# Turning paged keys on another engine: a decoder step's score stage rebuilt around a ring of sixteen half-page slots

## What is computed

```python
k_past = cache_k[page_table].reshape(nb, -1, N_HEADS, HEAD_DIM)     # 8 x 2048 x 16 x 64, fp32
v_past = cache_v[page_table].reshape(nb, -1, N_HEADS, HEAD_DIM)
F_all = cumsum(concatenate([lf_past, lf_s], axis=1), axis=1)
s = einsum('nqhd,nkhd->nhqk', q, k) * HEAD_DIM ** -0.5 + fq - fk
p = softmax(where(kpos <= qpos, s, -inf))
o = einsum('nhqk,nkhd->nqhd', p, v)
x = x + (o * silu(z)) @ w_out
```

## Time and profile before

| | |
|---|---|
| median of 3 runs | 979.52 us (976.55 to 979.72) |
| span of the profiled execution | 973.7 us, 23729 instructions |
| TensorE busy | 935.6 us, 96% |
| VectorE, ScalarE, GpSimd busy | 489.1, 384.8, 168.3 us |
| moved by DMA | 206.4 MB |

### The profile page before, as it was taken

The page is one execution under the profiler, slowest core; times in us unless marked ns, Lnnn a source line. Parts: engine busy times, 40 slices in busy tenths (PEclk is TensorE's granted clock), DMA queues, the critical chain, the costliest instruction groups (busy, mean ns, idle before and its releaser), DMA issues.

```text
span 973.7 us, 23729 instructions
## 1 busy us (share of the span) xinstructions
PE 935.6 (96%) x8516; PEld 798.8 (82%) x8516; DVE 489.1 (50%) x1133; ACT 384.8 (40%) x728; POOL 168.3 (17%) x111
## 2 busy tenths in 40 slices
PE   3899999999999999999999999999999999999998
PEld 2899999999998997758768768678687687786898
DVE  5744645555256434453554544644535545545732
ACT  5233333332135443453543544535435445436210
POOL 2243444331130221101102002012020020100000
PEclk8799999999999999999999999999999999999999
DMA  6222222322542525879799799798897997986412
GB/s 211 68 85 86 66 87 84 86 86 89 152 150 81 177 87 178 295 253 368 249 334 335 241 361 317 245 372 297 280 356 251 352 336 241 370 317 227 166 44 98
DMA packets 133188, 206.40 MB, mean 212 GB/s; under 512 B 8831, under 2 KB 91312, under 8 KB 133026
## 3 DMA queue, kind: packets, MB, share of 16 engines
q1 hardware_dynamic: 123538, 199.40, 60.7%
q10 hardware_dynamic: 9088, 4.46, 1.7%
q0 software_dynamic: 528, 2.10, 0.8%
HBM read 195.29 MB, written 10.63 MB: 211 GB/s over the span
## 4 chain that ended last, share of the span: by engine, by line
PE 84%; DMA 5%; DVE 4%; ACT 4%; issue 2%; SPq 0%; ACTq 0%; DVEq 0%
PE psum L1224 41%; PE psum L1194 17%; PE psum L1249 9%; PE psum L1382 7%; PE psum L1497 4%; DMA page_ring<-in_cache_k 4%; ACT sample_scores L708 2%; PE psum L1447 2%; DMA w_raw<-in_a_w_out 1%; PE psum L1425 1%; PE psum L1297 1%; PE psum L1405 1%; PE psum L1427 1%; PE psum L1429 1%; DMA constants<-in_table 0%
## 5 line engine op out<-in xcount | busy, mean ns | idle before, releaser
L1224 PE MATMUL psum<-xn_high,w_high 128*128 128x256 f32 x992 | 233.9, 318 | 2.6 <-DVE xn_low L821 2.6
L1224 PE MATMUL psum<-xn_low,w_high 128*128 128x256 f32 x992 | 213.6, 297 | 0.0
L1224 PE MATMUL psum<-xn_high,w_low 128*128 128x256 f32 x992 | 213.5, 297 | 0.0
L1224 PEld LDWEIGHTS psum<-xn_high,w_high 128*128 128x128 f32 x992 | 162.9, 191 | 19.6 <-issue 16.6
L1224 PEld LDWEIGHTS psum<-xn_high,w_low 128*128 128x128 f32 x992 | 168.1, 190 | 0.0
L1224 PEld LDWEIGHTS psum<-xn_low,w_high 128*128 128x128 f32 x992 | 168.0, 190 | 0.0
L1194 PE MATMUL psum<-constants,page_ring 128*128 128x128 f32 x1024 | 136.4, 276 | 6.3 <-DMA page_ring<-in_cache_k 5.0
L1194 PEld LDWEIGHTS psum<-constants,page_ring 128*128 128x128 f32 x1024 | 114.1, 140 | 33.4 <-issue 31.9
L503 POOL TENSOR_TENSOR w_raw<-w_raw,gains 128x1024 f32<-128x1024 f32 x32 | 60.7, 1897 | 339.2 <-DMA w_raw<-in_b_w_in 218.3
L1002 DVE COPY k_turned_odd<-psum 128x512 f32<-128x512 f32 x64 | 44.1, 690 | 93.1 <-PE psum L1194 93.1
L835 DVE TENSOR_TENSOR w_low<-w_raw,w_high 128x1024 fp32r<-128x1024 f32 x32 | 49.6, 1551 | 78.7 <-ACT w_high L565 78.7
(11 more groups left out here) (236 smaller groups left out, 1418.7 us busy)
## 6 DMA issues: line engine op xcount, KB each, us to landing
page_ring<-in_cache_k SPq DMA_DIRECT2D x128, 512.0 KB, 5.6
page_ring<-in_cache_v SPq DMA_DIRECT2D x128, 512.0 KB, 4.7
w_raw<-in_a_w_in SPq DMA_DIRECT2D x32, 512.0 KB, 4.0
suffix<-suffix_scratch SPq DMA_DIRECT2D x32, 256.0 KB, 4.6
w_raw<-in_b_w_in SPq DMA_DIRECT2D x16, 512.0 KB, 5.6
w_raw<-in_kv_w SPq DMA_DIRECT2D x16, 512.0 KB, 6.3
w_raw<-in_a_w_out SPq DMA_DIRECT2D x4, 1024.0 KB, 5.0
f_broad<-f_scratch SPq DMA_DIRECT2D x8, 512.0 KB, 6.0
```

Source lines behind the costliest of these rows:

```text
L1224: mm = pe.matmul(PS[:, bank + h, 0:c.stop - c.start], w[:, k, :], x[:, k, c], start=(k == 0 and n == 0), stop=(k == KT - 1 and n == 2))
```

## The change

- Key pages are no longer turned by PE. DVE turns them in place, in blocks of 32 x 32 (`turn_keys`), one instruction per ring slot.
- The ring has 16 slots. A key slot holds the same half (8 heads) of two pages, loaded by two DMAs of 256 KB with a page number read for each; slots 0 to 7 hold the first half of the heads of all 16 pages, 8 to 15 the second half. A value slot holds one page as before.
- Scores come in two rounds (`past_scores`) of 64 matmuls of 32 x 32 tiles, 512 columns wide, into four PSUM banks. ACT spreads the queries (`spread`). The suffix is loaded straight into `SS` in one DMA of 1 MB, and four adds put the scores on it in place.
- Value slots 0 to 7 wait for round 0 (`b_scored`), 8 to 15 for round 1. The gate weights are loaded behind key slot 13 of the previous head.
- The high and low parts of the gated outputs of the prompt are made in the last head for all heads, instead of in each head. Buffers are moved, the mask of the new keys is loaded at the end, the spread of the queries for the new keys is made by POOL at the end.

```diff
-RING = 8
+RING = 16
+HALF_D = D // 2
@@ SP
+        def load_keys(b, n, free=None):
+            pages = [page_of(b, 2 * (n % 8) + e) for e in range(2)]
+            if free:
+                sp.wait_ge(*free)
+            for e in range(2):
+                src = kpages[bass.ds(pages[e], 1), :, n // 8 * HALF_D:(n // 8 + 1) * HALF_D]
+                sp.dma_start(ring[:, n, e * HALF_D:(e + 1) * HALF_D],
+                             src.rearrange("a p n -> (a p) n")).then_inc(b_page[n], 16)
...
         def heads(i, last):
-            for n in range(STREAM):
...
+            sp.wait_ge(b_c0f, 4 * i)
+            sp.wait_ge(b_c1f, 4 * i)
+            src = f_dram[bass.ds(2 * i, 2), 0:SEQ].unsqueeze(0).to_broadcast([P, 2, SEQ])
+            sp.dma_start(FB[:, :, :], src).then_inc(b_fb, 16)
+            if not last:
+                sp.wait_ge(b_split, KT + 3 * i + 1)
+                load_w(wkv, (i + 1 + KT) * P, 0)
+            for n in range(NPG):
+                load_values(i, n, (b_scored, 2 * i + n // 8 + 1) if n % 8 == 0 else None)
+                if n == 7 and not last:
+                    sp.wait_ge(b_split, KT + 3 * i + 3)
                     load_w(wkv, (i + 1) * P, 1)
...
+            for n in range(NPG):
...
+                    load_keys(i + 1, n, (b_used, NPG * i + n + 1))
+                if n == 8:
+                    sp.wait_ge(b_t0, 8 * i + 4)
+                    sp.wait_ge(b_t1, 8 * i + 4)
...
+                        load_suffix(i + 1)
+                if n == 13 and not last:
+                    sp.wait_ge(b_split, KT + 3 * i + 5)
+                    load_w(wqz, (i + 1 + KT) * P, 1)
@@ ACT, heads
+            pr, sa = both(D0)
+            act.wait_ge(b_proj, KT + 3 * i + 1)
...
+            act.activation(SQ[:, SEQ:TOK], sa, ACT.Square).then_inc(b_dact, 1)
+            high_b(KT + 3 * i + 2, 1)
...
+            if last:
+                act.wait_ge(b_used, NPG * i + 10)
+                for k in range(KT - 1):
+                    act.activation(G2H[:, k, 0:SEQ], QF[:, k, 0:SEQ], ACT.Copy).then_inc(b_gh, 1)
@@ DVE
+        def turn_keys(b, n):
+            dve.wait_ge(b_page[n], 48 * b + 32)
+            dve.transpose(ring[:, n, :], ring[:, n, :]).then_inc(b_turned, 1)
+
+        for n in range(4):
+            turn_keys(0, n)
@@ DVE, heads
+            for n in range(4, 8):
+                turn_keys(i, n)
+            dve.wait_ge(b_proj, KT + 3 * i + 1)
+            pr, sa = both(D0)
...
+            dve.tensor_scalar(KN_T[:, SEQ:TOK], sa, gk, None, ALU.mult).then_inc(b_ddve, 1)
+            low_b(KT + 3 * i + 2, 1)
+            for n in range(8, NPG):
+                turn_keys(i, n)
...
+            for g in range(4):
+                ss = SS[:, :].rearrange("p (n g k) -> p n g k", g=4, k=32)[:, :, g, :]
+                dve.tensor_tensor_reduce(ss, PS[:, T0 + g, :].rearrange("p (n k) -> p n k", k=32), ss,
+                                         1.0, NEG, ALU.add, ALU.max, TINY[:, 4 + g:5 + g]).then_inc(b_taken, 1)
...
             block_turned(2)
+            if not last:
+                turn_keys(i + 1, 0)
             block_divide(3)
+            if not last:
+                turn_keys(i + 1, 1)
...
                 low_b(KT + 3 * i + 4, 1)
+                turn_keys(i + 1, 2)
+                turn_keys(i + 1, 3)
...
+            if last:
+                for k in range(KT - 1):
+                    low(k).then_inc(b_gl, 1)
@@ PE, heads
+            def past_scores(r):
+                half = ring[:, 8 * r:8 * r + 8, :].rearrange("p s (e c) -> p (s e) c", e=2)
+                for e in range(2):
+                    for a in range(2):
+                        for j in range(4):
+                            for g in range(4):
+                                h, c = 2 * r + e, ((2 * j + e) * 2 + a) * 32
+                                mm = pe.matmul(
+                                    PS[32 * j:32 * j + 32, T0 + g, :].rearrange("p (n k) -> p n k", k=32),
+                                    QC[32 * g:32 * g + 32, j, 64 * h + 32 * a:64 * h + 32 * a + 32],
+                                    half[32 * g:32 * g + 32, :, c:c + 32],
+                                    start=(h == 0 and a == 0), stop=(h == 3 and a == 1), tile_position=(32 * g, 32 * j))
+                mm.then_inc(b_scored, 1)
...
+            project(0, range(KT - 1))
...
+            pe.wait_ge(b_turned, NPG * i + 8)
+            project(0, [KT - 1])
+            past_scores(0)
+            project(1, range(1))
...
+            project(1, range(1, KT - 1))
+            pe.wait_ge(b_turned, NPG * i + NPG)
+            project(1, [KT - 1])
+            past_scores(1)
```

More of the change, by code:

```diff
@@ L188, in build @@
     CO = place("conv_rows", [18, D], over=at["probs_t"])
-    WHB = place("w_high_b", [P, KT, SLAB], F32R, over=at["k_turned"])
+    WHB = place("w_high_b", [P, KT, SLAB], F32R, over=slot(14))
     WLB = place("w_low_b", [P, KT, SLAB], F32R, over=at["p_turned"])
@@ L198, in build @@
     QF = place("queries", [P, KT, TOK], over=at["gated_high"])
+    QZ = place("q_spread", [P, NB, KT, 32], over=at["sample_scores"])
     FA = place("f_raw", [H, TOK], over=at["k_t"])
@@ L203, in build @@
     FT = place("f_sum", [H, TOK], over=at["f_broad"])
-    SN = place("new_scores", [P, NB, NS], over=at["suffix"])
-    NBI = place("new_bias", [P, NB, NS], over=at["suffix"] + 4 * NB * NS)
+    SN = place("new_scores", [P, NB, NS], over=at["new_keys"])
+    NBI = place("new_bias", [P, NB, NS], over=at["new_keys"] + 4 * NB * NS)
     PNT = place("new_probs_t", [NS, NB, P], over=at["probs"])
@@ L366, in _ @@
             load_w(wqz, n * P, n % 2)
+        sp.wait_ge(s_rows, 16 * 9)
+        sp.wait_ge(s_cs, H)
+        for n in range(2):
+            load_keys(0, n)
         for t in range(NT):
@@ L370, in _ @@
             sp.dma_start(h_dram[t * P:t * P + rows(t), :], X[0:rows(t), t, :]).then_inc(s_hst, 16)
+        for n in range(2, 7):
+            load_keys(0, n)
         sp.wait_ge(s_co, 1)
@@ L384, in _ @@
         sp.wait_ge(s_xl, 2 * NT)
-        for n in range(RING // 2):
-            load_page(0, n)
+        for n in range(7, 9):
+            load_keys(0, n)
         sp.wait_ge(s_ft, 1)
@@ L512, in heads @@
             scale_b(1, 6 + 2 * i, G_B)
-            if not last:
-                scale_b(0, 6 + i, G_KV)
             pool.wait_ge(b_rr, i + 1)
@@ L528, in _ @@
         heads(NB - 1, True)
+        pool.wait_ge(b_t0, 8 * (NB - 1) + 4)
+        pool.wait_ge(b_t1, 8 * (NB - 1) + 4)
+        pool.memset(QZ[:, :, :, :], 0.0).then_inc(s_zero, 1)
+        pool.wait_ge(s_zero, 2)
+        for e in range(2):
+            for s in range(2):
+                h = slice(64 * e, 64 * e + 64)
+                c = 16 * s + 8 * e
+                pool.tensor_copy(
+                    QZ[h, :, 4 * s:4 * s + 4, c:c + NQ],
+                    QF[h, 4 * s:4 * s + 4, SEQ:TOK].rearrange("p k (b q) -> p b k q", b=NB)).then_inc(b_qz, 1)
     @block.scalar
```

438 lines of the change are left out of this document (191 added, 247 removed).

## The result

The changed kernel takes 1066.11 us (median of 4 runs, 1064.21 to 1067.57), the kernel before 978.03 beside it (4 runs, 973.26 to 979.72): a ratio of 1.0908, 95% interval 1.0876 to 1.0941. The forecast was 1006, its range 950 to 1045: the direction was right, the size was not, by 60 us. The profiled execution has a span of 1062.4 us.

A forecast was written before the change was run, and what follows sets the result against it. TensorE bounds the old loop; after the change a circle of waits through SP and the gate weights would. 403.4 + 7 x 70.0 + 28.4 + 73.0 + 5.9 = 1000.7 us span, plus 5.8 around it: 1006 us, range 950 to 1045.

The forecast's parts named there:

- the circle of one head: Loop over heads: waits through SP, gate weights, turns and round 1 close a loop, 70.0 us per head against 66.4.
- The step that failed: From the end of round 1 until value page 0 has been used: 9.5 us before, 0.9 more, so 10.4.
- SP's cost per slot: SP queue: a key slot takes two page number reads and two DMA issues, 2.45 us, bounds 2.3 to 2.5.
- The turn: VectorE's in-place turn of one 128 x 1024 key slot: 1.22 us, taken from an fp32 SBUF row.
- The round: TensorE's 64 score matmuls, two passes each, all 16 tiles running together: 3.56 us including 0.15 for the mode change.
- TensorE's need: TensorE's work per head falls from 66.4 to 50.4 us, so something else becomes the bound.
- Ahead and behind: Outside the loop: first round 1 ends at 403.4 us; after the last, 28.4, then 73.0, plus 5.9 for late low parts.
- The signs: Trace marks: 2.45 us slots, gate-weight wait, gapless turns, 15 to 20 us TensorE idle, clock dip, 3.6 us rounds.
- The first: Rival 1: TensorE's clock stays up since rounds and projections are dense enough, 67.2 us per head, 985 us; chance 0.17.
- The second: Rival 2: SP overlaps second read with first issue, slot 1.24 us, DMA bounds at 59.1 per head, 929 us; chance 0.10.
- The third: Rival 3: VectorE's turn moves two elements a cycle, 0.61 us, 44 us less, 962 us; chance 0.08.
- fourth: Rival 4: turn takes two passes, 2.44 us, 1094; or 4 x 4 tiles don't overlap in rows, 1098; chance 0.15 together.

The follow-up runs named there:

- Both experiments: Changed kernel with the value weights' high part early on ScalarE (1019.09 us), or their low part behind VectorE's copies of turned probabilities and the sum (1014.73 us).
- the orders are mended: Changed kernel with value weights' high part early, gate weights loaded behind key slot 8, and their low part made behind the turns: 967.66 us.
- numbers held: Kernel with those three order edits, SP also keeping page numbers of key slots 0 to 7 in registers for slots 8 to 15: 947.12 us.
- one read: Changed kernel with the second page number of each key slot left out, both halves loaded from the same page: 1040.23 us.
- the matmuls against the low clock: Changed kernel with six additional matmuls of 512 columns in TensorE's idle time ahead of each second round, result unused: 1068.10 us.
- as the third: Gate weights' low part made behind turns 8 to 15: 1009.54 us alone on the changed kernel, 967.66 us added to the other two order edits.
- the 80 waits: Kernel with page numbers held in registers, plus 80 waits on an already raised semaphore in SP's program of each head: 962.11 us.

## Why the prediction was wrong, and where it was right

Its steps against the trace, for the circle of one head:

| step of the circle | forecast, us | measured, us |
|---|---|---|
| end of round 1 until value page 0 is used, SP goes on | 10.4 | 19.7 (557.5 to 577.2) |
| key slot 0 to the gate weights' issue | 33.9 | 32.4 (to 609.6) |
| weights landing, with waits | 4.2 | 6.6 (to 616.2) |
| scale, high part, low part | 4.5 | 4.2 (to 620.3) |
| eight turns | 9.8 | 9.1 (to 629.5) |
| piece, round 1, low clock | 7.2 | 7.0 (to 636.5) |
| sum | 70.0 | 79.0 |

Over all seven heads the means are 20.2, 32.8, 5.4, 4.2, 9.1 and 7.2 us, in the same order. So the first step is 9.8 us over, and the others together 0.9 under.

**The step that failed is the first one**, "until value page 0 has been used: 9.5 us today ... so 0.9 more: 10.4". It took the stretch from the kernel before and added what the change does to the suffix adds, but it didn't look at what else the change had moved *into* that stretch on ScalarE. The two kernels have it in plain view, though the excerpt of the diff ahead of the prediction doesn't show it: `high_b` of the value weights now stands behind three DMA issues. The prediction costed the orders on SP, and the gate weights' order on VectorE, and passed over this one because the weights themselves aren't needed for another 40 us. What mattered is what stands behind the waiting instruction on VectorE. Both experiments put the term at 7 to 8 us per head. The rest, 2 us, is what the stretch still has over the 10.4 forecast when the wait is gone (12.4 and 12.2 us in the two kernels). With the wait, the idle time also leaves a low clock: the first value page takes 1.08 us, against 0.64 in the earlier trace rows.

**SP's cost per slot** came out a little under 2.45 us: slots 0 to 8 are issued 2.37 us apart (577.21 to 596.17 in eight steps), slots 9 to 13 2.20 apart (599.38 to 608.17 in four). The bounds were 2.3 to 2.5. This and the turns made the circle shorter by 1.8 us in the mean of the heads, and the landing of the weights took 1.2 of it back: 4.7 to 6.6 us, in the mean 5.4, instead of 4.2 with the waits. The mixer's 4.0 were measured where the DMA engines are at two or three tenths.

**The turn** on VectorE was right: 1.21 us each, 1.14 apart, where 1.22 was taken from the fp32 row of the same size. The Trainium skill (Vector Engine (DVE) Microarchitecture Reference, section 3.8) gives one element per cycle and lane; the trace fits that in so far as the turn takes what the low split of the same 1024 columns takes, 1.21 us.

**The round** takes 4.47 us at full clock, where 3.56 was forecast: the tiles do overlap both ways (four column tiles alone would have taken 13.7), but it is 0.9 us slower than full overlap. The forecast's 0.15 for the change of mode is shown by no row. The Trainium skill (TensorE: Matmul & The Clock Gate, Part 3: Packing small matmuls) gives a factor of 10.6, an estimated 5.2 us; the measured round lies halfway, an estimate of 128 x 0.427 / 4.47 = 12.2 times, and the measurement decides. On the circle this cancelled against the low clock, forecast at 2.8 and measured at 1.7: two errors of opposite sign, so that 7.2 us came out right is luck. TensorE's need, forecast at 50.4 us per head, is 55.8 in the trace; the two rounds are 2.7 of the difference, the rest wasn't followed up. It isn't on the circle.

**Ahead and behind** were right. Round 1 of head 0 ends at 401.3 (403.4 forecast, 401.9 without low clock; it ran at full clock, 4.47 us). Behind the last round the first value page comes after 11.0 us (9.8), the sixteen take 18.5 (18.6), and from 983.3 the end is 79.1 away (78.9), with the seven high and low parts just where they were put: the slab's low part is ready 9.1 us behind the last value page, 9.8 forecast. ScalarE and VectorE there:

```profile
981.49 1.90 ACT L633 ACTIVATE w_high<-w_raw 128x2048 fp32r<-128x2048 f32 x1
983.29 3.73 ACT L832 ACTIVATE gated_b_high<-queries 128x512 fp32r<-128x512 f32 x7
...
990.16 2.28 DVE L925 TENSOR_TENSOR w_low<-w_raw,w_high 128x2048 fp32r<-128x2048 f32 x1
```

**The signs** that it named for the circle were there: the wait for the gate weights' high part, eight turns without a gap, the dip of the clock, a DMA share of 0.78 at 264 GB/s. Three sizes were off: the rounds took 4.47 us and not 3.6, the slots 2.2 to 2.4 and not 2.45, and TensorE stood idle for 13.4 us ahead of the second round and not 15 to 20. None of the signs could have told that the circle had a second stall. Only a forecast of *where TensorE stands idle in all* would have: 19 us in one place were forecast, 13.4 and 6.8 in two places came.

**The rivals.** The first (the clock stays up) is out: the second rounds start at 1.2 GHz, at a price of 1.7 us per head. The second (a slot at 1.24) didn't occur, but its bound, the DMA engines, is what is nearly full once the orders are mended and the numbers held. The third and fourth are out by the rows of the turn and the round. The point from which the second rival "wins over the old kernel", a slot cheaper than 2.17 us, was wrong: with one read a slot costs 1.70 to 1.76 us, and the kernel still takes 1040 us, since the missed wait stays and the weights land later. With the orders mended the change wins with slots of 2.2 to 2.4 (968 us).

## What to carry to other kernels

When a change moves an instruction on one engine, list who waits for its result, and then what stands *behind that waiter* in its own program: the price is that of the work behind, not of the result, which may be needed much later. A result that nobody needs soon (the low part of the next head's weights) belongs behind the work that is due, on both engines. To tell a circle of waits from a full engine, double a piece of work: on a circle it costs its full length in one place and nothing in another. Look at every head of the trace before calling an edit without effect: the matmuls against the low clock shortened the loop and cost as much in head 0. And mended stalls add up only until the next resource is full, so expect each further edit to be worth less (9.0 us per head alone, 0.8 as the third).

## What the runs showed of the hardware

SP's jump back at the end of its loop costs 0.3 us while the loop's body is 283 instructions (the kernel before), 274 (one read) or 298 (numbers held), and 3.0 to 5.8 us with 338 (the 80 waits) or 346 (two reads): the trace counts the instructions between two jumps. The short ones have 13 or 14 packets in the instruction queue on the page, the long ones 44 or 45. Where between 298 and 338 the step lies wasn't measured. The Trainium skill (Runtime: NRT & Kernel Launch, Instruction fetch mechanics) says that instructions are fetched ahead in sequence, and that a taken branch to one outside of what is held stops the engine until its block has been fetched. The trace agrees with this in that the long gaps and the additional packets come together; it adds the price, 3.0 to 5.8 us. The jump can have cost the change itself little, since its SP waits for 15.6 us in the head shown anyway (566.3 to 577.2 and 631.9 to 636.6), but it was a part of the last 20 us on the way to 947.

An issue is not a landing: the same 512 KB of gate weights landed 5.4 us after their issue in the mean of seven heads in the changed kernel, 10.2 when they were issued 0.9 us behind the suffix, and 9.4 when they were issued 9.2 us behind it; the suffix of 1024 KB takes 8.5 to 10.3 us itself (medians of the three kernels). In the changed kernel the weights are issued 12.2 us behind the suffix (597.37 and 609.58), when it has landed. That it was the suffix that held them fits all three, but wasn't tested alone. Bringing an issue forward by 7.9 and by 11.5 us brought its data forward by 4.0 and 6.8.
